# Expert step and sorting stage of a fused two-block kernel, in another order

## The reference, cut to what matters

```
h = layer_norm(ALPHA * h + mix)
group = argmax(h @ router_group_w + b)               # 1 of 4 groups
two experts of that group's 4, with gates            # combine: 512 x 16
y = sum over e of ((silu(h @ w_gate[e]) * (h @ w_up[e])) * combine[:, e]) @ w_down[e]     # w_gate, w_up 1024 x 256, w_down 256 x 1024
out = layer_norm(ALPHA * h + y)
```

## Time and profile before

| | before |
|---|---|
| median of 3 runs | 2966.44 us (2964.28 to 2969.91) |
| profiled execution, device time | 2964.72 us |
| its span | 2962.9 us |
| busy in the span | PE 2655.6, PEld 2238.0, DVE 1207.5, ACT 699.6, POOL 1384.7 us |
| mean granted PE clock | 0.944 |
| sorting stage, last router part to first expert matmul | 2598.50 to 2641.74 us |
| expert steps, first to last matmul | 2641.74 to 2947.3 us |
| DVE's `lo` (L3205) | 84 times, 2286 ns each |
| ACT's `hi` (L3141) | 84 times, 1911 ns each |

### The profile page before, as it was taken

How to read it: one execution, slowest core, us unless ns; L and a number is a source line. 1 busy time by engine, 2 the same in 40 slices (tenths; PEclk the granted TensorE clock), 3 DMA queues, 4 the chain that set the end, 5 groups by cost and what they waited for, 6 DMA issues and landing times. The chain is left out here.

```text
span 2962.9 us, 35922 instructions
## 1 busy us (share of the span) xinstructions
PE 2655.6 (90%) x14316; PEld 2238.0 (76%) x14316; DVE 1207.5 (41%) x1694; ACT 699.6 (24%) x1130; POOL 1384.7 (47%) x435
## 2 busy tenths in 40 slices
PE   4999999987999979987999989989989999948886
PEld 3888888875898848875888867878878978936665
DVE  4102011225774623067111233454332166278885
ACT  3111001012211411102100113433421111146664
POOL 2433555442552027674778764745447767210000
PEclk7999999997999989998999988989999999869998
DMA  5443121123221022231223224210022223447873
GB/s 229 192 193 139 68 71 57 53 104 125 72 70 46 1 87 85 85 128 57 85 83 109 86 84 157 85 37 1 1 100 100 100 101 116 165 189 310 326 303 121
DMA packets 52302, 334.96 MB, mean 113 GB/s; under 512 B 6501, under 2 KB 7525, under 8 KB 19345
## 3 DMA queue, kind: packets, MB, share of 16 engines
q1 hardware_dynamic: 50592, 327.44, 29.9%
q0 software_dynamic: 1584, 5.78, 0.5%
HBM read 314.84 MB, written 22.07 MB: 114 GB/s over the span
## 5 line engine op out<-in xcount | busy, mean ns | idle before, releaser
L160 POOL TENSOR_TENSOR whi<-raw,one_col 128x2048 fp32r<-128x2048 f32 (+2 forms) x160 | 533.4, 3334 | 949.8 <-PE bank L180 718.0
L163 POOL TENSOR_TENSOR wlo<-raw,whi 128x2048 fp32r<-128x2048 f32 (+2 forms) x160 | 708.0, 4425 | 12.5
L178 PE MATMUL bank<-uh_a,whi 128*128 128x512 f32 (+1 forms) x704 | 239.0, 339 | 14.6 <-DVE ul_a L600 14.6
L179 PE MATMUL bank<-ul_a,whi 128*128 128x512 f32 (+1 forms) x704 | 237.6, 337 | 0.0
L180 PE MATMUL bank<-uh_a,wlo 128*128 128x512 f32 (+1 forms) x704 | 237.2, 337 | 0.0
L3205 DVE TENSOR_TENSOR moe_wl<-moe_raw,moe_wh 128x2048 fp32r<-128x2048 f32 x84 | 191.1, 2286 | 26.9 <-ACT moe_wh L3141 26.5
L3141 ACT ACTIVATE moe_wh<-moe_raw 128x2048 fp32r<-128x2048 f32 x84 | 160.2, 1911 | 27.3 <-PE bank L3116 26.3
L3053 POOL DMA_INDIRECT out_dram<-moe_y,moe_rows x7 | 17.3, 2468 | 306.0 <-DVE moe_y L3262 306.0
L178 PEld LDWEIGHTS bank<-uh_a,whi 128*128 128x128 f32 x704 | 134.1, 190 | 34.3 <-issue 16.9
L178 PE MATMUL bank<-uh_b,whi 128*128 128x512 f32 x352 | 137.9, 392 | 7.6 <-DVE ul_b L600 6.6
L180 PEld LDWEIGHTS bank<-uh_a,wlo 128*128 128x128 f32 x704 | 134.0, 190 | 14.1
(11 more groups left out here) (550 smaller groups left out, 6467.3 us busy)
## 6 DMA issues: line engine op xcount, KB each, us to landing
moe_raw<-moe_w_dram SPq DMA_DIRECT2D x84, 1024.0 KB, 6.8
cond_ring<-w_ada_dram SPq DMA_DIRECT2D x27, 1024.0 KB, 7.2
raw<-gu_a_dram SPq DMA_DIRECT2D x22, 1024.0 KB, 5.2
raw<-gu_b_dram SPq DMA_DIRECT2D x22, 1024.0 KB, 4.8
raw<-wqkv_dram SPq DMA_DIRECT2D x12, 1024.0 KB, 4.7
raw<-dn_a_dram SPq DMA_DIRECT2D x16, 704.0 KB, 4.0
raw<-dn_b_dram SPq DMA_DIRECT2D x16, 704.0 KB, 4.0
ada_w<-w_ada_dram SPq DMA_DIRECT2D x9, 1024.0 KB, 20.1
```

The source lines that it names most:

```text
L160: e.nc.gpsimd.tensor_tensor(e.whi[p][:, 0:f], e.raw[p][:, 0:f], e.one_col[:, 0:1].to_broadcast([P, f]), ALU.mult).then_inc(e.w_hi, 1)
L163: e.nc.gpsimd.tensor_tensor(e.wlo[p][:, 0:f], e.raw[p][:, 0:f], e.whi[p][:, 0:f].bitcast(F32), ALU.subtract).then_inc(e.w_split, 1)
L178: e.nc.tensor.matmul(out, wh, xh, start=first, stop=False)
L179: e.nc.tensor.matmul(out, wh, xl, start=False, stop=False)
```

## The change

Expert step. ACT: `x_hi` stands first in its iteration, and `root` after `hi` D. DVE: `x_lo` stands first in its iteration; `lo` of a D slot stands one iteration later, right after `hidden_lo`; `centre` runs in the iteration after (x % 4 == 2). SP: `XB` of block b is asked for three slots later than before: after the weights of A(4b), B(4b) and D(4b-1), not ahead of them. It still waits for `evacuate(b-2)`.

Sorting stage. The first pass of rows 0, 1 and 2 runs before the wait for PE's last router part; that of row 3 after the experts' choice; the second pass of all four rows after `dest` and the gates. The logits of the chosen group take 2 operations in place of 7. PE adds the counts of earlier tiles to the ranks itself (three more small matmuls). `dest` takes 15 operations in place of some 33. What only `gsel` needs is in `dve_groups`, after the rows, with its own semaphore, for which SP waits. DVE waits for all four scatters before its first `lo`, and does `lo` 0 to 2, `x_lo(0)`, `lo` 3 to 5 (before: `lo` 0 to 3, `x_lo(0)`, `lo` 4 and 5).

```diff
@@ OutRows.dve_logits
         link(nc.vector.reciprocal(self.rs[:, :], self.sd[:, :]))
+        self.dve_rows_first(dve, tok, (0, 1, 2))
         dve.wait_ge(self.routed, 4)
@@ Grouping.pe_count
-        nc.tensor.matmul(e.bank[4][:, 0:16], self.TRI[:, :], mg, start=True, stop=True)
+        nc.tensor.matmul(e.bank[4][:, 0:16], self.TRI[:, :], mg, start=True, stop=False)
+        for t in range(NCH - 1):
+            nc.tensor.matmul(e.bank[4][:, 4 * t + 4:16], e.ones[:, :],
+                             self.MG[:, t, :].unsqueeze(1).to_broadcast([P, NCH - 1 - t, 4]),
+                             start=False, stop=t == NCH - 2)
@@ Grouping.dve
         first_max(MG, lg, M1, self.mg_ready)
-        self.late.dve_rows(dve, self.tok, (0, 1))
...
+        link(V.tensor_tensor(ig, LG[:, :, 4:4 + 4 * EPG].rearrange("p t (g x) -> p t g x", g=4),
+                             MG[:, :, :].unsqueeze(3).to_broadcast([P, NCH, 4, EPG]), ALU.mult))
+        link(V.tensor_reduce(IN[:, :, :], self.IG[:, :, :].rearrange("p t (g x) -> p t x g", g=4), AX, ALU.add))
...
-        self.late.dve_rows(dve, self.tok, (2, 3))
+        self.late.dve_rows_first(dve, self.tok, (3,))
...
+        V.tensor_copy(self.dest[:, :], self.D1[:, :, 0]).then_inc(self.dest_ready, 1)
...
+        V.tensor_tensor(self.tok[:, :, D:D + 4], CI[:, :, :], wide(W1[:, :, :]), ALU.mult).then_inc(self.rec_ready, 1)
+        self.late.dve_rows_second(dve, self.tok)
@@ block.sync
-                if kind == "A" and x % EPG == 0 and b >= 2:
-                    sp.wait_ge(evac_done, b - 1)
-                    sp.wait_ge(rows_done, b - 1)
-                    sp.dma_start(XB[b % 2][:, :], e.dram["xs"][b * P:(b + 1) * P, :]).then_inc(xb_in[b % 2], 16)
...
-                        sp.wait_ge(route.dest_ready, 1)
+                        sp.wait_ge(route.gsel_ready, 1)
...
+                if kind == "D" and x % EPG == EPG - 1 and 2 <= b + 1 < NBLK:
+                    sp.wait_ge(evac_done, b)
+                    sp.wait_ge(rows_done, b)
+                    sp.dma_start(XB[(b + 1) % 2][:, :], e.dram["xs"][(b + 1) * P:(b + 2) * P, :]
+                                 ).then_inc(xb_in[(b + 1) % 2], 16)
@@ block.scalar
             for x in range(NSTEP + 1):
+                if x % EPG == EPG - 1 and x // EPG + 1 < NBLK:
+                    x_hi(x // EPG + 1)
                 if x:
                     hidden(x - 1)
...
                     hi(slot["B", x + 2])
+                if x + 1 < NSTEP:
+                    hi(slot["D", x + 1])
                 if x % EPG == 1 and x > EPG:
                     root(x // EPG - 1)
-                if x % EPG == EPG - 1 and x // EPG + 1 < NBLK:
-                    x_hi(x // EPG + 1)
-                if x + 1 < NSTEP:
-                    hi(slot["D", x + 1])
@@ block.vector
-            for n in range(4):
+            route.dve_groups(dve)
+            dve.wait_ge(scattered, 16 * NCH)
+            for n in range(3):
                 lo(n)
             x_lo(0)
-            for n in range(4, RING_W):
+            for n in range(3, RING_W):
                 lo(n)
             for x in range(NSTEP + 1):
+                if x % EPG == EPG - 1 and x // EPG + 1 < NBLK:
+                    x_lo(x // EPG + 1)
                 if x:
                     hidden_lo(x - 1)
+                if 0 < x < NSTEP:
+                    lo(slot["D", x])
                 if 0 < x < NSTEP - 2:
                     lo(slot["A", x + 2])
...
                     lo(slot["B", x + 2])
-                if x % EPG == EPG - 1 and x // EPG + 1 < NBLK:
-                    x_lo(x // EPG + 1)
-                if x + 1 < NSTEP:
-                    lo(slot["D", x + 1])
                 if x % EPG == 0 and x:
                     normalise(x // EPG - 1)
-                if x % EPG == 1 and x > EPG:
+                if x % EPG == 2 and x > EPG:
                     centre(x // EPG - 1)
```

More of the change, by code:

```diff
@@ L2754, in dve_low, with dve_logits @@
                                                   ).then_inc(self.lo_ready, 1)
-    def dve_logits(self, dve, LG):
+    def dve_logits(self, dve, LG, tok):
         nc, e = self.e.nc, self.e
@@ L2773, in dve_logits, with dve_rows_first @@
         link(nc.vector.tensor_tensor(LG[:, :, :], LG[:, :, :], wide(1), ALU.add))
-    def dve_rows(self, dve, tok, ts):
+    def dve_rows_first(self, dve, tok, ts):
         nc = self.e.nc
@@ L2781, in dve_rows, with dve_rows_second @@
                                            ALU.subtract, ALU.mult).then_inc(self.half_row, 1)
-        for t in ts:
+    def dve_rows_second(self, dve, tok):
+        for t in range(NCH):
             dve.wait_ge(self.half_row, t + 1)
-            nc.vector.scalar_tensor_tensor(tok[:, t, 0:D], tok[:, t, 0:D], self.rs[:, t:t + 1], self.LN1[:, D:2 * D],
-                                           ALU.mult, ALU.add).then_inc(self.row_ready, 1)
+            self.e.nc.vector.scalar_tensor_tensor(tok[:, t, 0:D], tok[:, t, 0:D], self.rs[:, t:t + 1],
+                                                  self.LN1[:, D:2 * D], ALU.mult, ALU.add).then_inc(self.row_ready, 1)
 class Grouping:
@@ L2806, in __init__ @@
         self.TRI = self.st.sb("tri", [P, P], MAIN + 140032)
-        self.CNT, self.PRE, self.PM, self.NT = (small(n, NCH, 4) for n in ("cnt", "pre", "pm", "nt"))
-        self.RK, self.D0, self.D1, self.LT, self.DF = (small(n, NCH, 1) for n in ("rk", "d0", "d1", "lt", "df"))
-        self.X1, self.X2, self.EE, self.EB, self.B1 = (small(n, 1, 4) for n in ("x1", "x2", "ee", "eb", "b1"))
+        self.PM, self.GT, self.IG = small("pm", NCH, 4), small("gt", NCH, 4), small("ig", NCH, 4 * EPG)
+        self.D1 = small("d1", NCH, 1)
+        self.NT, self.X1, self.X2, self.EE, self.EB, self.C0, self.DB = (
+            small(n, 1, 4) for n in ("nt", "x1", "x2", "ee", "eb", "c0", "db"))
         self.LE, self.GB = small("le", 3, 3), small("gb", 3, 1)
@@ L2812, in __init__ @@
         self.const_in, self.e1_pre, self.e1_ready, self.e2_pre, self.e2_ready, self.mg_ready, self.count_psum, \
-            self.dest_ready, self.rec_ready, self.chain = (
+            self.dest_ready, self.rec_ready, self.gsel_ready, self.chain = (
                 self.st.sem(n) for n in ("const_in", "e1_pre", "e1_ready", "e2_pre", "e2_ready", "mg_ready", "count_psum",
-                                         "dest_ready", "rec_ready", "chain"))
+                                         "dest_ready", "rec_ready", "gsel_ready", "chain"))
+        self.late_chain = self.st.sem("late_chain")
     def sp(self, sp):
@@ L2886, in dve @@
         dve.wait_ge(self.const_in, 64)
-        self.late.dve_logits(dve, LG)
+        V.tensor_scalar(self.C0[:, 0, :], self.BASE0[:, :], -1.0, 384.0, ALU.mult, ALU.add)
+        V.memset(self.EB[:, :, :], 0.0)
+        self.late.dve_logits(dve, LG, self.tok)
         lg = LG[:, :, 0:4]
@@ L2891, in dve @@
         first_max(MG, lg, M1, self.mg_ready)
-        self.late.dve_rows(dve, self.tok, (0, 1))
-        dve.wait_ge(self.e1_ready, 1)
-        link(V.tensor_reduce(GP[:, :, :], EX[:, :, :], AX, ALU.add))
-        for n in range(4):
[L2897 to L2900, removed]
+        ig = self.IG[:, :, :].rearrange("p t (g x) -> p t g x", g=4)
+        link(V.tensor_tensor(ig, LG[:, :, 4:4 + 4 * EPG].rearrange("p t (g x) -> p t g x", g=4),
+                             MG[:, :, :].unsqueeze(3).to_broadcast([P, NCH, 4, EPG]), ALU.mult))
+        link(V.tensor_reduce(IN[:, :, :], self.IG[:, :, :].rearrange("p t (g x) -> p t x g", g=4), AX, ALU.add))
         link(V.tensor_reduce(M1[:, :, :], IN[:, :, :], AX, ALU.max))
@@ L2904, in dve @@
         link(V.tensor_reduce(W2[:, :, :], IN[:, :, :], AX, ALU.max))
+        V.tensor_tensor(SM[:, :, :], W2[:, :, :], M1[:, :, :], ALU.subtract).then_inc(self.e2_pre, 1)
         first_max(MB, IN[:, :, :], W2)
-        V.tensor_tensor(SM[:, :, :], W2[:, :, :], M1[:, :, :], ALU.subtract).then_inc(self.e2_pre, 1)
-        self.late.dve_rows(dve, self.tok, (2, 3))
+        self.late.dve_rows_first(dve, self.tok, (3,))
         dve.wait_ge(self.count_psum, 1)
         rank = e.bank[4][:, 0:16].rearrange("p (t g) -> p t g", g=4)
-        link(V.tensor_copy(self.CNT[:, :, :], e.bank[5][:, 0:16].rearrange("p (t g) -> p t g", g=4)))
@@ L2912, in dve @@
[L2912 to L2917, removed]
-        link(V.tensor_tensor(self.PM[:, :, :], self.PM[:, :, :], MG[:, :, :], ALU.mult))
@@ L2919, in dve @@
[L2919 to L2925, removed]
@@ L2926, in dve @@
-        link(V.tensor_tensor(self.EB[:, :, :], self.EE[:, :, :], self.X1[:, :, :], ALU.subtract))
+        counts = e.bank[5][:, 0:16].rearrange("p (t g) -> p g t", g=4)
+        link(V.tensor_reduce(self.NT[:, 0, :], counts, AX, ALU.add))
+        link(V.tensor_scalar(self.X1[:, :, :], self.NT[:, :, :], 128.5, None, ALU.is_gt))
+        link(V.scalar_tensor_tensor(self.X2[:, :, :], self.NT[:, :, :], 256.5, self.X1[:, :, :], ALU.is_gt, ALU.add))
```

(30 more changed lines are left out.)

## The result

The kernel after took 2900.11 us (median of 4 runs, 2896.1 to 2901.78) against 2965.36 before: ratio 0.9775 (95% interval 0.9758 to 0.9792), 65 us less; the forecast was 2906. The profiled execution spans 2897.5 us against 2962.9.

The account below looks back on a forecast made before the run. No engine filled a block; PE's waits, ended by DVE's order, set its length. Terms 13.5 + 4.0 + 36.8 + 5.8 = 60.1 took the span from 2962.9 to 2902.8, median 2906 us; range 2899 to 2924.

Parts of the forecast that it names:

- sorting stage, to PE's first matmul: Before the experts: earlier gates and faster scatters let PE begin at 2628.2 instead of 2641.74, -13.5 us (-10.8 at other end).
- block 0: First expert block: stall at its end goes (3.1), `lo` D no longer precedes its first `hidden_lo` (0.9): -4.0 us.
- blocks 1 to 5: Steady expert blocks: 36.8 us each, 184.0 in place of 220.8 us, -36.8 us.
- last block: Last expert block: loses both D stalls (3.6, less 0.4) and most of the clock's 3.2 us: -5.8 us.
- The walk through the queues: Steady block, step by step through ACT's and DVE's lists: 36.4 us, DVE full, PE 1.4 behind its own 35.0.
- I add 0.4, half of what I could not place above: Steady block: half of the old block's unplaced 0.75 us added to the walk's 36.4, giving 36.8 us.
- (1) DMA: Steady blocks: DMA becomes the bound at about 38.8 us each, +10 us, 2916; chance 0.13.
- (2): Expert blocks: clock falls on short stalls too, +9 us, 2915; against it, no fall at 2753.04 after 1.84 us; chance 0.10.
- (3): Steady blocks: `centre` and `x_lo` together hold `hidden_lo` for 3 us, not 1; +2 for five blocks, 2916; chance 0.10.
- (4): Before the experts: the sorting stage or the scatters give half, +7 us, 2913; chance 0.05.
- (5): Five blocks: `XB` lands late, so PE, ACT and DVE stand still; slower than before if landing exceeds 21 us; chance 0.04.
- the 3.13 us: PE's stall before A of each new block: goes with `x_lo` moved first, and the clock fall behind it (1.3 us).

Follow-up runs that it names:

- e_nowait: The kernel after without DVE's wait for the scatters before its first three `lo`: ratio 0.9785, start 31.99 us against 29.85.
- e_light: The kernel after with `centre`'s first pass cut to 64 of 1024 columns in all blocks but the last: steady block 35.18 us, ratio 0.9755.
- e_xbold: The kernel after with the load of `XB` asked for where it was before, ahead of A(4b): steady block 36.19 us, ratio 0.9774.
- e_split: The kernel after with `centre`'s second pass moved to the end of the next iteration: steady block 36.04 us, ratio 0.9784.
- e_xonly: The kernel before with only `x_hi` and `x_lo` moved to the front of their iteration: steady block 40.4 us, ratio 0.9908.

## Why the prediction was right or wrong

The mechanism held and the size did not: 60.1 us were forecast and 65.5 measured, and each of the three terms of the expert steps was too small. Term by term, in the profiled executions:

| term (us) | forecast | measured |
|---|---|---|
| sorting stage, to PE's first matmul | -13.5 | -12.8 (-13.4 from the logits on) |
| block 0 | -4.0 | -5.3 |
| blocks 1 to 5 | -36.8 | -40.2 |
| last block | -5.8 | -7.2 |
| sum | -60.1 | -65.5 |

**Sorting stage: right in each step.** Logits 0.2 late by forecast; one-hot to gates, first scatter at 12.9 from the logits' start in place of 24.1, landing 8.9 later (forecast 8.4; the second issue, beside the second passes, took 1.90 and not 0.95). e_nowait shows the scatter step by itself. The first matmul came at 2628.95 for 2628.2.

**Steady block: mechanism right, size off.** The walk through the queues gave 36.4 with DVE full and 1.4 us of PE stalls; measured 36.19, 35.95 and 1.1. What failed is "I add 0.4, half of what I could not place above". The rest of 0.75 was never unplaced: a block of before is PE's busy 36.9 and stalls of 3.13, 1.9 and 1.84, and that is all 43.85. The fall of the clock had been priced too low, 1.3 for a window of 2.93 us where it lasts 3.41 at 0.50 and costs 1.7, and the third stall at 1.8 for 1.9; the other 0.2 or so are PE's slower first matmuls behind each wait. All of it goes with the stalls, so none had a place in the new sum. (The 28.5 us of the earlier trace rows are idle time of PE's weight loads; PE's own stalls before D were 25.1.) That 0.4 is 2 of the 3.4 us missed in blocks 1 to 5; 1.0 more is the walk's 0.2 per block, and 0.4 that block 1 took 35.83, as DVE entered it on time.

**Block 0 and the last block: under-credited.** Both gains, 5.3 and 7.2, lie outside the ranges of their terms (3.1 to 4.6, 3.2 to 6.4). In block 0 the stall before its first D, booked at 0.9, was 1.53 and went; PE's busy time fell by another 0.7, about half of it because the clock rose 4.3 us in and not 4.8. In the last block the stalls gave 3.8 where I had booked 3.2, and PE's busy time fell by 3.5 (40.86 to 37.31), where I had booked 2.6 for the clock.

**The range.** Its low end, 2899, took DVE's sum as the floor for five blocks and allowed 1 to 3 us elsewhere. Three of the four sizes erred to the same side, 6.1 us together, and the sorting stage gave back only 0.7, so the time came out at its very edge: the median is 2900.11, and 0.9775 of 2965.36 is 2898.6. That it still came so near the low end was luck in part, since the sorting stage erred the other way.

**Rivals.** (1) DMA: share 0.96, longest landing of a weight slot 10.9 us, no wait of ACT for it; e_light and e_xbold settle it. The Trainium skill's DMA page ("Specifications") has some 358 GB/s of HBM per core; the runs gave 384 over a block of e_light, so it did not bind here. (2) The clock did not fall on stalls of 0.9 us, nor anywhere on one of 1.54 or less. But "nothing fell at 2753.04" was half of the record: in the kernel before it fell behind the same kind of stall, 1.91 us, in block 3, which is why that block took 45.4, and again in the last (PE's row, and the window of that fall with the columns as above).

```profile
2786.38 0.64 PE L3114 MATMUL bank<-moe_wh,moe_hh 128*128 128x512 f32 x1 [1.91 <-issue]
2786.52:2789.93 3.41, 3.41 (x9) 2.64 (x10) 3.41 (x3) 1.75 (x3) 0.00 (x0) 0.50 1.01 428
```

(3) The wait behind `centre` and `x_lo` was 0.91; e_split, where it is gone and one of 1.15 stands elsewhere, gains 0.15 a block. (4) The sorting stage gave 12.8 of 13.5. (5) `XB` landed within 8.3 us; nobody waited.

**A claim that I had wrong without a price.** I had the fall of the clock go with the 3.13 us, by the move of `x_lo`. In e_xonly that stall is gone and the clock falls all the same, in four blocks of five, behind stalls of 1.84 and 1.92 that are left. The fall goes only when `lo` D moves too, so the two moves aren't two separate cures.

## What to carry to other kernels

In a loop shared by three engines, write each engine's start-to-start times from the trace and walk its list through one period: the sum of the fullest list and the chain of the others are two separate floors, and an edit that lowers one does nothing while the other is as high. Split a block into an engine's busy time and its stalls before you call anything a rest: what was left here stood in PE's busy time, as a price of the clock. Don't carry an unexplained rest over to a loop with a new bound. Judge small edits by the mean block in the profile, which repeated within 0.02 us in the kernel after, not by the whole time, and look at the first and the last block as well.

## What the runs showed of the hardware that I had not expected

POOL's issue of an indirect DMA took 0.95 us with DVE idle and 1.69 to 2.69 beside its `lo`, which reads two operands from SBUF. A delivery took 3.08 us in the loop before, where it ran beside `lo`, 5.29 in e_split, beside two of them, and 0.95 in the loop after, beside `x_lo`, which reads one operand from PSUM; no other engine waits for it. The Trainium skill's SBUF page ("Who interferes with whom") has a DVE instruction with two SBUF inputs contend with a GpSimd instruction that reads SBUF, which would fit, since the issue reads its row numbers (`moe_dest`, `moe_rows`) from SBUF, though no run shows that apart; but it infers that such an instruction doesn't hold up the making of descriptors, and has them locked out by DVE's 2-port modes, which `lo`'s operation lacks. The runs show the slower issue all the same, so the agreement that I noted in the prediction is with the durations, not with that rule as the page has it.

TensorE's granted clock fell to 0.50 at every stall of 2.77 us or more in the experts' blocks, at some of those of 1.75 to 1.93 and at none of 1.54 or less. Why two stalls of the same 1.9 us differ in this was not tried.

The spread of the whole time (2895 to 2904 us for the kernel after) does not come from the part that was changed: the logits began anywhere from 2595.4 to 2604.0 us in the profiles, though in the kernel after and its variants everything ahead of them is the same code, while the 29.8 us of the start and the 36.19 of a block repeated. Why the earlier stages vary was not tried.
